# A block layer's first products taken ahead of the norm: feed-forward input and sparse layers fed with the not yet normalised residual

## The reference, cut to what matters

```
x = x + rms_norm(memory_cross_attention(h, mem_n, w_xq, w_xkv, w_xo), norm_x_post)   # norm 4
h = rms_norm(x, norm_ff_pre)                                                          # norm 5
f = jnp.square(jax.nn.relu(h @ w_ff1)) @ w_ff2
x = x + rms_norm(f, norm_ff_post)                                                     # norm 6
...
for l in range(2):                                    # two sparse layers
    h = rmsnorm(x, norm_g_2[l])                       # norm 7, norm 8
    z = h @ w_in_2[l]
    ...                                               # branches, attention, merge
    x = x + merged @ w_out_2[l]
return rmsnorm(x, final_norm_g_2)                     # norm 9
```

## Time and profile before

| | |
|---|---|
| median of 3 runs | 2371.65 us (2371.1 to 2377.44) |
| the profiled execution, its own time | 2360.77 us |
| its span in the profile | 2359.1 us |
| PE busy | 2195.1 us, 93% of the span |
| DVE, ACT, POOL busy | 1089.6, 1012.7, 825.2 us |
| PE's mean granted clock | 0.970 |

### The profile page before, as it was taken

One profiled execution on the slowest core, in us unless ns is written; L12 is line 12 of the kernel. 1 busy time (PEld: TensorE's weight loads), 2 busy tenths in 40 slices (PEclk: granted clock), 3 DMA queues, 4 the chain that ended last, 5 costly groups with the idle time before them and its releaser, 6 DMA issues.

```text
span 2359.1 us, 31769 instructions
## 1 busy us (share of the span) xinstructions
PE 2195.1 (93%) x11292; PEld 1802.0 (76%) x11292; DVE 1089.6 (46%) x1934; ACT 1012.7 (43%) x1919; POOL 825.2 (35%) x364
## 2 busy tenths in 40 slices
PE   5988888799998997999999999999998999999997
PEld 4777777687888786888887787777777787777776
DVE  5689899525344245423225433222355543222364
ACT  5756666645234343423222433443642433444631
POOL 2422222134446322444442333333343433333342
PEclk9999999989999997999998899999999999999999
DMA  3221121132334211333332322222232322222231
GB/s 140 81 63 49 49 62 49 54 98 81 98 98 133 82 46 36 98 98 95 94 96 63 111 90 72 72 65 71 73 97 81 112 81 81 68 67 72 73 97 63
DMA packets 51741, 189.41 MB, mean 80 GB/s; under 512 B 6564, under 2 KB 7204, under 8 KB 51108
## 3 DMA queue, kind: packets, MB, share of 16 engines
q1 hardware_dynamic: 48096, 175.13, 24.9%
q10 hardware_dynamic: 2452, 6.88, 0.8%
q0 software_dynamic: 1072, 5.77, 0.6%
HBM read 185.66 MB, written 2.10 MB: 80 GB/s over the span
## 4 chain that ended last, share of the span: by engine, by line
PE 71%; DVE 13%; issue 5%; ACT 5%; DVEq 4%; POOL 2%; DMA 0%; ACTq 0%; POOLq 0%
PE bank L337 20%; PE bank L338 19%; PE bank L339 19%; PE bank L869 2%; PE bank L912 2%; POOL weight_lo L368 1%; PE bank L895 1%; DVE attention_work L1606 1%; ACT wide_region L994 1%; ACT weight_hi L363 1%; DVE wide_region L1987 1%; PE bank L411 1%; DVE work_region L1630 1%; DVEq L1572 1%; DVE wide_region L1990 1%
## 5 line engine op out<-in xcount | busy, mean ns | idle before, releaser
L368 POOL TENSOR_TENSOR weight_lo<-weight_slots,weight_hi 128x1024 fp32r<-128x1024 f32 x286 | 691.0, 2417 | 1103.2 <-ACT weight_hi L363 1103.2
L363 ACT ACTIVATE weight_hi<-weight_slots 128x1024 fp32r<-128x1024 f32 x286 | 302.6, 1059 | 825.9 <-PE bank L339 754.2
L337 PE MATMUL bank<-h_hi,weight_hi 128*128 128x512 f32 x1248 | 507.4, 407 | 20.6 <-DVE h_lo L385 12.6
L338 PE MATMUL bank<-h_lo,weight_hi 128*128 128x512 f32 x1248 | 492.1, 394 | 0.0
L339 PE MATMUL bank<-h_hi,weight_lo 128*128 128x512 f32 x1248 | 491.9, 394 | 0.0
L337 PEld LDWEIGHTS bank<-h_hi,weight_hi 128*128 128x128 f32 x1248 | 237.4, 190 | 76.0 <-DVE h_lo L385 15.2
L339 PEld LDWEIGHTS bank<-h_hi,weight_lo 128*128 128x128 f32 x1248 | 237.5, 190 | 51.6
L338 PEld LDWEIGHTS bank<-h_lo,weight_hi 128*128 128x128 f32 x1248 | 238.4, 191 | 43.9
L368 POOL TENSOR_TENSOR head_weight_lo<-weight_slots,head_weight_hi 128x1024 fp32r<-128x1024 f32 x42 | 104.3, 2485 | 293.0 <-ACT head_weight_hi L363 293.0
L337 PE MATMUL bank<-h_hi,head_weight_hi 128*128 128x512 f32 x336 | 139.3, 415 | 5.5 <-DVE h_lo L385 3.0
L338 PE MATMUL bank<-h_lo,head_weight_hi 128*128 128x512 f32 x336 | 132.8, 395 | 0.0
(11 more groups left out here) (439 smaller groups left out, 4275.9 us busy)
## 6 DMA issues: line engine op xcount, KB each, us to landing
weight_slots<-weights SPq DMA_DIRECT2D x328, 512.0 KB, 3.6
wide_region<-cmp_w ACTq DMA_DIRECT2D x2, 2048.0 KB, 8.2
v_region<-ssm_bc POOLq DMA_DIRECT2D x8, 256.0 KB, 4.8
residual<-x_in POOLq DMA_DIRECT2D x1, 2048.0 KB, 9.2
out<-normed SPq DMA_DIRECT2D x4, 512.0 KB, 2.7
residual<-x_in SPq DMA_DIRECT2D x2, 512.0 KB, 5.7
residual<-x_in ACTq DMA_DIRECT2D x2, 512.0 KB, 10.1
v_region<-mem_in POOLq DMA_DIRECT2D x1, 1024.0 KB, 5.1
```

Source lines behind the costliest of these rows:

```text
L337: pe.matmul(to, w_h[:, k, :], hi[:, k, 0:width], start=(k == 0), stop=False)
L338: pe.matmul(to, w_h[:, k, :], lo[:, k, 0:width], start=False, stop=False)
L363: act.activation(parts[0][s % 2], slot[s], ACT.Copy).then_inc(w_hi[s], 1)
L368: eng.tensor_tensor(parts[1][s % 2], slot[s], parts[0][s % 2].bitcast(F32), ALU.subtract).then_inc(w_lo[s], 1)
```

## The change

At A, B and C the first products take `X * gain` as input, which needs no root. The root is multiplied onto the products afterwards.

- **A.** DVE's loop over k adds the cross attention to X and, two steps behind, makes `h_lo` of `X * gain`; ACT makes `h_hi` of it and the square of X. Before: two loops with norm 5 between them. PE runs blocks 0, 1 and 2 of quad `Q_FF` into banks 0, 1 and 2 side by side: for each k nine matmuls, then the four one-column matmuls of norm 5. Block 3 goes into bank 3, with the spread of norm 5 in its middle. Three more pairs of weight buffers (`W_FF`) hold the quad. POOL makes three `weight_lo` ahead of the power of norm 4, and now waits for the root (`rstd_ready`) before the fourth.
- **Feed-forward.** `h` stays without its root for all 8 input quads. DVE, not ACT, takes each of the 32 hidden blocks out of PSUM as `max(., 0) * root`, squares it and makes the rest; ACT keeps the rounding of the square.
- **B.** The same for quad `Q_L2`, with two blocks side by side (six matmuls and the sums of norm 7 for each k), then blocks 2 and 3. Their input is `scaled_hi`/`scaled_lo`. The rest of the layer still takes the fully normed `h_hi`/`h_lo`, which DVE makes meanwhile.
- **C.** Here the sums stay together, ahead of k = 6 of block 0, and blocks 0 to 3 go one after the other. DVE and ACT make `scaled_lo` and `scaled_hi` within the loop over the last output blocks.
- DVE takes the four blocks of the layers' first quad out of PSUM (`scaled_out`) in place of ACT. The layer loop is written out twice. The layer vectors are loaded at the start and within the layer before.

```diff
+            for k in range(KT):
+                pe.wait_ge(lo_ready, S_HF + k + 1)
+                for s in range(3):
+                    mm = ff_terms(s, k)
+                    if k == KT - 1:
+                        mm.then_inc(mm_done[s], 1)
+                pe.wait_ge(sq_ready, 5 * KT + (k + 1))
+                mm = norm_terms(pe, k, k == 0, k == KT - 1, TT, SQ)
+            mm.then_inc(ms_ready, 1)
+            pe.wait_ge(w_lo[3], Q_FF + 1)
+            for k in range(KT):
+                if k == KT // 2:
+                    norm_spread(pe, 5)
+                mm = ff_terms(3, k)
+            mm.then_inc(mm_done[3], 1)
...
+            for L in range(LAYERS):
+                q0 = QL * L + Q_L2
+                for s in range(2):
+                    pe.wait_ge(evac_done[s + 2], q0)
+                if L == 0:
+                    pe.wait_ge(var_ready, 7)
+                    for s in range(2):
+                        pe.wait_ge(w_lo[s], q0 + 1)
+                    for k in range(KT):
+                        pe.wait_ge(lo_ready, S_L2 + S_T + (k + 1))
+                        for s in range(2):
+                            scaled_terms(s, k)
+                        pe.wait_ge(sq_ready, 7 * KT + (k + 1))
+                        mm = norm_terms(pe, k, k == 0, k == KT - 1, TT, SQ)
+                    mm.then_inc(ms_ready, 1)
+                else:
+                    pe.wait_ge(w_lo[0], q0 + 1)
+                    for k in range(KT):
+                        pe.wait_ge(lo_ready, SL * L + S_L2 + S_T + (k + 1))
+                        if k == KT - 2:
+                            norm_sums(pe, L + 7, L + 6)
+                        scaled_terms(0, k)
+                    pe.wait_ge(w_lo[1], q0 + 1)
+                    for k in range(KT):
+                        if k == KT // 2:
+                            norm_spread(pe, L + 7)
+                        scaled_terms(1, k)
+                pe.wait_ge(w_lo[2], q0 + 1)
+                for k in range(KT):
+                    if L == 0 and k == KT // 2:
+                        norm_spread(pe, L + 7)
+                    scaled_terms(2, k)
+                pe.wait_ge(w_lo[3], q0 + 1)
+                for k in range(KT):
+                    scaled_terms(3, k)
+                pe.wait_ge(evac_done[0], q0 + 1)
+                gemm(pe, q0 + 1, 0, H_HI, H_LO, T, SL * L + (S_L2 + S_H), own_bank=True)
...
+                act.activation(H_HI[:, k, :], X[:, k, :], ACT.Copy, scale=column(V_FF_PRE + k)).then_inc(hi_ready, 1)
+                act.activation(SQ[:, k, :], X[:, k, :], ACT.Square).then_inc(sq_ready, 1)
...
                 for k in range(KT):
+                    if L == 0 and k == 2:
+                        weight_hi(act, q0 + 1, 0)
                     round_hi(act, stages + S_H, k, H_HI[:, k, :], H[:, k, :])
+                if L > 0:
+                    weight_hi(act, q0 + 1, 0)
+                weight_hi(act, q0 + 1, 1)
...
+                if 1 <= k <= KT:
+                    dve.tensor_tensor(X[:, k - 1, :], X[:, k - 1, :], YB[:, k - 1, :], ALU.add).then_inc(x_ready, 1)
+                dve.drain()
+                if k >= 2:
+                    dve.wait_ge(hi_ready, S_HF + (k - 1))
+                    dve.scalar_tensor_tensor(H_LO[:, k - 2, :], X[:, k - 2, :], column(V_FF_PRE + (k - 2)),
+                                             H_HI[:, k - 2, :].bitcast(F32), ALU.mult, ALU.subtract).then_inc(lo_ready, 1)
...
+                dve.wait_ge(mm_done[s], quad + 1)
+                dve.scalar_tensor_tensor(RELU[s % 2], src[:, :], 0.0, RELU[2],
+                                         ALU.max, ALU.mult).then_inc(evac_done[s], 1)
+                dve.drain()
+                dve.tensor_tensor(f, RELU[s % 2], RELU[s % 2], ALU.mult)
+                dve.drain()
+                dve.wait_ge(ff_hi, 4 * i + (KT * c + s + 1))
+                dve.tensor_tensor(f_lo, f, one(F_HI[c % 2], 4 * i + s).bitcast(F32), ALU.subtract).then_inc(ff_lo, 1)
...
+                dve.wait_ge(bc_ready, L + 8)
+                dve.tensor_copy(TOKENS, bank[7][:, :])
...
+                if L == 0:
+                    scaled_out(0)
+                    scaled_out(1)
                 norm_split(dve, L + 7, stages + S_H, H, H_HI, H_LO, X, LVEC[:, L_NORM:L_NORM + KT])
+                for s in range(2 if L == 0 else 0, 4):
+                    scaled_out(s)
```

245 lines of the change are left out of this document (179 added, 66 removed).

## The result

The changed kernel takes 2345.67 us (median of 4 runs, 2342.72 to 2346.07), the kernel before 2371.38 us in the same comparison (4 runs). The ratio is 0.9893 (95% interval 0.9878 to 0.9908): 25.7 us or 1.1% less, where I had forecast 11 us less. That is close to the first rival's 2344.6 us.

The account below looks back on a forecast made before the run. PE's products were taken as the bound, with norms between them. A +10.5, B -9 and C +9.5 made 11 us less: from the median 2371.65 to 2360.6 us, range 2342 to 2369.

Parts of the forecast that it names:

- A: Gap at norms 4 and 5: clock back within two k, mixed stretch 27.5 us, gain 10.5 us.
- C: Start of the second layer: gain 9.5 us, upper bound the whole gap of 13.5 plus 3 us, lower bound 3.
- Feed-forward: The 32 hidden blocks: DVE needs 4.5 us of a block's 5.4, PE waits for nothing, cost nothing.
- the first rival: The clock comes back at B too: B gives 7 us, total 27 us less, 2344.6 us; chance 0.28.
- I take the low level for the whole stretch: Step at B: products and sums all run at half clock, 34.2 us.
- that is shorter than the shortest run behind which the trace shows the clock back (3.4 us): Ground for the low clock at B: its runs of products last only 2.6 us.
- B's term: Quad Q_L2 with two blocks side by side, at the low clock: costs 9 us.
- within two k: Other end at B: clock back within two k, stretch 21.7 us, B gives 7 us.
- The list of signs: Expected in the changed profile; at A, clock 0.50 for 3 to 7 us of products, then 1.00.
- if the clock falls, 2 to 3 us less: At C, PE idles 2.7 us ahead of block 0; a third chance of a fall costing 2 to 3 us.
- It comes back at neither: Second rival: clock stays low at A and B, A's stretch 44.5 us, 2378 to 2380 us; chance 0.09.
- Small waits in the feed-forward part: Third rival: DVE or a weight_lo late, ten waits of 1 us leave nothing, about 2370 us; chance 0.09.

Follow-up runs that it names:

- e3: Changed kernel, but at B the sums of a k are halved: three products, two one-column matmuls, twice; 2360.7 us, ratio 0.9963 to the kernel before.
- e2: Kernel before with only the parts at B and C, written-out layer loops and earlier vector loads; 2359.13 us, ratio 0.9958.
- e5: Changed kernel, but at A the sums of a k are divided among the blocks, so runs of three products, not nine; 2345.16 us, ratio 0.9893.
- e4: Changed kernel, but at B the four one-column matmuls of each k are issued twice, first into a spare bank; 2347.3 us, ratio 0.9913.
- e9: e3 with one useless product-sized matmul behind each run of three products at B; 2354.67 us, ratio 0.9938 to the kernel before.
- e6: Changed kernel, but at B the products of two k are taken together, then their sums: runs of twelve; 2342.48 us, ratio 0.9889.
- e10: Changed kernel, but at B all sums of norm 7 stand behind the 48 products; 2345.92 us, ratio 0.9912 to the kernel before.
- e8: Changed kernel with useless matmuls in PE's waits at A, B and within layers; second layer's first full block made ready sooner; 2328.18 us, ratio 0.9821.
- e12: e8 with 11 more useless matmuls at C, where the second layer's first products wait for weights; 2326.31 us, ratio 0.9820 to the kernel before.
- e11: Kernel before, its real work in the same order, with useless product-sized matmuls at A, B and C; 2375.69 us against 2367.39, ratio 1.0038.
- e1: Kernel before with only the part at A and the feed-forward part; 2360.72 us against 2370.42, ratio 0.9959.

## Why the prediction was wrong

**The step that failed** is B's: "I take the low level for the whole stretch". It rested on "that is shorter than the shortest run behind which the trace shows the clock back (3.4 us)". A shortest run that one trace happens to show is no lower bound. With runs of 2.6 us the clock rose in all three traces of the changed kernel's code at B (after 7.7, 11.3, 15.9 us). The price I had put on the low stretch was right (e3: 34.1 us, B -6.9); it was the wrong case. B's term is +7.2 in place of -9, 16.2 us more; with C's 2.1 less that is 14.1 of the 14.7 us by which the forecast missed. The first rival had it, with +7, at a chance of 0.28. Its "within two k" is what this one trace shows. In e2's and e5's, with the same code, B gave 5.6 and 3.6 us, so that the number agrees to 0.2 us is luck.

What decides is narrower than either theory that I took to the runs. At B, with one and the same work, the clock rose with runs of six and did not with runs of three (e3): the order counts, and both the traces and the times show it. The run of three alone doesn't decide either, since at A the clock rose with it, after 4.8 us where runs of nine took 8.5 to 9.4 in seven executions (e5). With runs of six it rose though products were less of the work (e4). That a larger part of products was what helped in e5 at A and in e9 is argued, not shown: in e5 the breaks are shorter too, and in e9 the runs longer. The quick return in e6 and e10 (4.5 and 4.8 us) fits longer runs, but each is one execution, and one and the same code waited from 7.7 to 15.9 us. Why it did so these runs don't settle.

**A** was right in its sum. The loop on DVE starts 7.6 us behind the last product's start (forecast 8.0), PE's first product another 4.6 us later (4.5), DVE's pace is 2.10 us a k (2.17), the stretch 27.9 us (27.5), the gain 10.6 (10.5). The slow DVE operation is gone (0.17 us at 900.33), since POOL's `weight_lo` no longer lies over it. Part of that is paid back: POOL's power starts 1.3 us behind DVE's operation at 897.81 that it needs (before 0.1), because POOL is still at the two `weight_lo`:

```profile
894.20 5.13 POOL L378 TENSOR_TENSOR ff_weight_lo<-weight_slots,ff_weight_hi 128x1024 fp32r<-128x1024 f32 x2
897.81 0.16 DVE L448 TENSOR_SCALAR small<-bank 128x4 f32<-128x4 f32 x1 [3.02 <-PE bank L421]
899.29 1.00 POOL L459 TENSOR_TENSOR small<-small 128x4 f32<-128x4 f32 x1
900.33 0.17 DVE L450 TENSOR_TENSOR small<-small 128x4 f32<-128x4 f32 x1 [2.36 <-POOL small L459]
```

The low clock lasted 8.9 us. The list of signs had "3 to 7", the sum had one and a half slow k, 1.5 x 5.6 = 8.4 us; the two don't fit together, and the sum was the right one. Products were unbroken for 3.9 us at a time there, longer than the 3.4 us of my rule, and still the first such run went by; the clock rose at the end of the second.

**Feed-forward** at nothing was right: PE has no idle time in 304.6 us. DVE is busy for 135.5 of them. Its longest operation for a hidden block is L1941, with two inputs in SBUF and a mean of 2.55 us:

```profile
L1941 DVE TENSOR_TENSOR ff_lo<-wide_region,ff_hi x24 | 61.2, 2551 | 6.1 <-ACT ff_hi L1338 6.1
L1935 DVE SCALAR_TENSOR_TENSOR attention_work<-bank,attention_work 128x512 f32<-128x512 f32 x26 | 18.0, 692 | 34.5 <-PE bank L348 34.5
```

Like L1880 of the earlier trace rows (2.73 us) it has both inputs in SBUF. L1941 took 0.69 us at 942.06, with no `weight_lo` beside it, and 2.73 us from 944.21, where a `weight_lo` ran from 943.73 to 946.39; it ended 0.55 us behind that one. The rule of the Trainium skill (SBUF — State Buffer, Who interferes with whom), that the later of two such instructions waits for the other's whole length, agrees. It cost nothing because 0.69 + 0.69 + 2.55 us is still less than a block's 5.4.

**C** gave 7.4 us, forecast 9.5. The first product came 2.95 us behind the last one's start, at 1.00 (forecast 2.5 to 3), and `norm_split` 15.0 us behind it (14.7). What I had too short was its end, by 0.9 us: ACT rounds the next weight only when all eight normed blocks are done, POOL follows, and PE's next product starts at 1834.16, 3.4 us behind the one before it and 31.0 us behind the last product of the layer before (30.1):

```profile
1830.58 1.99 ACT L372 ACTIVATE weight_hi<-weight_slots 128x1024 fp32r<-128x1024 f32 x2
1831.70 4.70 POOL L378 TENSOR_TENSOR weight_lo<-weight_slots,weight_hi 128x1024 fp32r<-128x1024 f32 x2 [7.94 <-ACT weight_hi L372]
```

Behind that wait the clock fell for 3.4 us (the window 1834.90), 1.6 us lost. I had "if the clock falls, 2 to 3 us less" as a third of a chance. It did fall, but not where that term stood, at the 2.7 us ahead of block 0: the windows show 1.00 there, and the fall behind a wait for which the sum had no clock loss. e8 takes the wait away and C gives 10.5.

**The sum.** With B's term right and the others as forecast it would have been 27; the profiles show 25.2 at the three places and the runs 25.7. "It comes back at neither" fell at A at once, with its 27.9 us. Small waits in the feed-forward part fell with its 304.6 us.

## What to carry to other kernels

The price of products laid into a norm's gap hangs on the clock level more than on anything in them (at B 22 us or 34 for the same instructions in another order), so put the products in long runs with the one-column matmuls in lumps between them (e10, with all of them at the end, took 4.5 us more at B), and take no bound for it from the one case that a trace happens to show. Where PE must wait some us between products, matmuls between constants into a spare bank together with one weight made ready sooner (e8's C is 3.1 us shorter than the changed kernel's) bought 17 us here (e12); too few of them between short instructions on the path only cost their length (e11). Compare stretches between fixed blocks, not spans, since the rest, with the same work in all kernels, took 459.7 to 465.0 us.

## What was not expected of the hardware

- The time until the clock rises varies widely for the same instructions: 7.7, 11.3 and 15.9 us at B. At A it was steadier: 8.5 to 9.4 us with runs of nine in the seven executions that have that code without useless matmuls at A (the changed kernel, e1, e3, e4, e6, e9, e10), and 4.8 with runs of three in the one of e5. The Trainium skill (TensorE: Matmul & The Clock Gate, Part 1: The HAM clock gate) says that the number of slow matmuls at a cold start varies from run to run of one kernel. The spread here agrees in kind; for products broken by one-column matmuls it was up to 15.9 us, and in e3 it did not rise in 34.
- PE was busy without a break in e3's stretch and the clock still stayed at 0.50 for all of its 34.1 us. A busy PE in the profile does not mean the high level.
- Idle times of 1.4 to 3.0 us between products were followed by a fall in some executions (those that end at 1834.16, 1936.93 and 2284.57 in the changed kernel, 3.03, 1.37 and 2.07 us long) and not in others (at 1959.66 and 2304.23 in the kernel before, 1.36 and 2.07 us); 3.4 us at 0.50 cost 1.7.
